# Down projection of a convolutional FFN: 18 of its 22 feature tiles by Strassen's seven products

## The reference

```python
def conv_ffn(x, w_up, conv_w, conv_b, w_down):
    h = x @ w_up                               # 1024 -> 2 * 2816
    h = depthwise conv of width 3 over tokens + conv_b
    a, u = jnp.split(h, 2, axis=-1)
    return (gelu(a) * u) @ w_down              # 2816 -> 1024

x = layer_norm(ALPHA * x + mix, ln1_g, ln1_b)
x = layer_norm(ALPHA * x + conv_ffn(x, ...), ln2_g, ln2_b)
```

## Time and profile before

| what | value |
|---|---|
| time, median of 3 runs | 1003.73 us (1003.02 to 1004.0) |
| span of the profiled execution | 1001.4 us |
| instructions in it | 12301 |
| PE busy | 987.4 us, 99% of the span |
| DVE, ACT, POOL busy | 734.4, 464.8, 220.7 us |
| mean granted TensorE clock | 0.999 |
| moved by DMA | 102.11 MB |

### The profile page before, as it was taken

How to read it: one execution, slowest core, us unless ns; L and a number is a source line. 1 busy time by engine, 2 the same in 40 slices (tenths; PEclk the granted TensorE clock), 3 DMA queues, 4 the chain that set the end, 5 groups by cost and what they waited for, 6 DMA issues and landing times.

```text
span 1001.4 us, 12301 instructions
## 1 busy us (share of the span) xinstructions
PE 987.4 (99%) x4614; PEld 824.2 (82%) x4614; DVE 734.4 (73%) x1110; ACT 464.8 (46%) x742; POOL 220.7 (22%) x210
## 2 busy tenths in 40 slices
PE   7999999999999999999999999999999999999997
PEld 6888888998888788888888888888888888888885
DVE  6664567886786898788778778778777394665587
ACT  6574666896313754554554554454457402113000
POOL 2400426774950000000000000000000299500022
PEclk9999999999999999999999999999999999999999
DMA  8334141008240223223222322322339512413022
GB/s 309 95 81 151 43 107 43 1 1 252 85 148 22 84 65 103 82 68 93 76 85 76 92 85 67 103 85 63 105 134 350 209 72 97 169 53 158 1 84 84
DMA packets 91179, 102.11 MB, mean 102 GB/s; under 512 B 20091, under 2 KB 71247, under 8 KB 91120
## 3 DMA queue, kind: packets, MB, share of 16 engines
q1 hardware_dynamic: 89904, 99.15, 30.0%
q10 hardware_dynamic: 1216, 2.17, 0.7%
HBM read 79.29 MB, written 22.02 MB: 101 GB/s over the span
## 4 chain that ended last, share of the span: by engine, by line
PE 95%; DVE 2%; ACT 2%; issue 1%; DMA 0%; POOL 0%; DVEq 0%; SPq 0%; ACTq 0%; POOLq 0%
PE ps L701 31%; PE ps L703 30%; PE ps L702 30%; PE ps L915 1%; PE ps L1044 1%; DVE prob L1377 1%; DVE pTl L1174 1%; ACT prob L1908 1%; PE ps L736 1%; ACT pTh L1731 0%; DMA acc<-in_x_prompt 0%; PE ps L711 0%; PE ps L724 0%; PE ps L884 0%; PE ps L976 0%
## 5 line engine op out<-in xcount | busy, mean ns | idle before, releaser
L701 PE MATMUL ps<-d_hi,g_hi 128*128 128x512 f32 x352 | 137.0, 389 | 0.0
L703 PE MATMUL ps<-d_hi,g_lo 128*128 128x512 f32 x352 | 136.9, 389 | 0.0
L702 PE MATMUL ps<-d_lo,g_hi 128*128 128x512 f32 x352 | 136.9, 389 | 0.0
L668 POOL TENSOR_TENSOR acc<-acc,gain_bc 128x1024 f32<-128x1024 f32 x12 | 32.8, 2732 | 466.2 <-ACT bias_bc L1731 466.2
L702 PEld LDWEIGHTS ps<-d_lo,g_hi 128*128 128x128 f32 x352 | 66.1, 188 | 13.8
L703 PEld LDWEIGHTS ps<-d_hi,g_lo 128*128 128x128 f32 x352 | 66.1, 188 | 13.8
L701 PEld LDWEIGHTS ps<-d_hi,g_hi 128*128 128x128 f32 x352 | 66.1, 188 | 13.7 <-DVE d_lo L1174 0.2
L701 PE MATMUL ps<-x1h,wa_hi 128*128 128x512 f32 x192 | 75.6, 394 | 0.0
L703 PE MATMUL ps<-x1h,w_lo 128*128 128x512 f32 x192 | 74.8, 389 | 0.0
L702 PE MATMUL ps<-x1l,wa_hi 128*128 128x512 f32 x192 | 74.7, 389 | 0.0
L2028 ACT ACTIVATE hc<-U,taps 128x512 f32<-128x512 f32 x60 | 48.7, 813 | 44.7 <-DVE U L1556 41.4
(11 more groups left out here) (298 smaller groups left out, 2740.4 us busy)
## 6 DMA issues: line engine op xcount, KB each, us to landing
w_raw<-in_w_up SPq DMA_DIRECT2D x44, 512.0 KB, 4.7
g_scratch<-gated SPq DMA_DIRECT2D x22, 512.0 KB, 2.6
g_raw<-g_scratch SPq DMA_DIRECT2D x22, 512.0 KB, 6.1
d_raw<-in_w_down SPq DMA_DIRECT2D x22, 512.0 KB, 7.4
acc<-in_x_sample SPq DMA_DIRECT2D x8, 512.0 KB, 12.0
st_raw<-in_w_in SPq DMA_DIRECT2D x16, 256.0 KB
x_scratch<-acc SPq DMA_DIRECT2D x8, 512.0 KB, 3.5
acc<-x_scratch SPq DMA_DIRECT2D x8, 512.0 KB, 7.9
```

What stands on the lines that cost most here:

```text
L668: chain.mark(pool.tensor_tensor(dst, dst, gain_bc[:], ALU.mult))
L701: pe.matmul(out, whi, xhi, start=start, stop=False, skip_group_check=onto)
L702: pe.matmul(out, whi, xlo, start=False, stop=False, skip_group_check=onto)
L703: return pe.matmul(out, wlo, xhi, start=False, stop=stop, skip_group_check=onto)
```

## The change

For the first 18 feature tiles the down projection is no longer 16 blocks per chunk. The tiles are taken in pairs (one tile is the first, the other the second half of the contraction), the tokens in two sequences and the columns in two halves, so that a pair is a product of 2 x 2 blocks, and it is done by seven products (`PRODUCTS`). Three pairs go together (`CHUNK` = 3), which gives 21 steps (`STEPS`). A step is four token tiles of nine matmuls, in four banks; even and odd steps use different banks. The products' operands are sums: those of gated rows (S1 to S4) are built in DRAM, in `gs_scratch`, and those of weights (T1 to T4) in `ts_scratch`, by transfers that POOL issues and that add to what their target holds (`accum_op`). Plain copies of the first terms are issued by SP. Each step loads 128 x 1536 of either operand into one of five slots (`SLOTS`). The last four tiles (`LAST`) are done as before, in 16 blocks of 12 matmuls.

Added or rewritten, cut to the core:

```diff
+PAIRED = 18
+QUADS = PAIRED // 2
+CHUNK = 3
+STEPS = 7 * (QUADS // CHUNK)
+SLOTS = 5
+LAST = FT - PAIRED
+PRODUCTS = ((X11, B11, True, True), (X12, B21, False, True), (S2, T2, False, False), (S1, T1, False, True),
+            (S3, T3, True, False), (S4, B22, False, False), (X22, T4, True, False))
+TARGETS = ((0, 0, 1), (0, 0, 1), (0, 1, -1), (4, 1, 1), (4, 1, -1), (0, 1, 1), (4, 0, 1))
+def by_act(n):
+    return n in (0, 2, 3, 6)
...
             def store_gated(v):
+                g, q = gated[v % 2], v // 2
                 sp.wait_ge(g_ready, 2 * v + 2)
-                sp.dma_start(g_dram[v], gated[v % 2][:]).then_inc(g_out[v % 2], 16)
...
+                elif v % 2 == 0:
+                    sp.dma_start(gs_dram[X11:S3 + 1, :, q, :].rearrange("i p n -> p i n"),
+                                 g[:, 0:SEQ].unsqueeze(1).to_broadcast([P, 3, SEQ])).then_inc(g_out[0], 16)
+                    sp.dma_start(gs_dram[S1, :, q, :], g[:, SEQ:2 * SEQ]).then_inc(g_out[0], 16)
...
+            def load_step(n):
+                c, i = divmod(n, 7)
+                a, w, s = PRODUCTS[i][0], PRODUCTS[i][1], n % SLOTS
...
+                if n >= SLOTS:
+                    sp.wait_ge(dn_ps, 4 * (n - SLOTS + 1))
+                sp.dma_start(ga_raw[s][:], gs_dram[a, :, quads(c), :]).then_inc(step_in[s], 16)
+                src = ts_dram[TSUM[w], :, quads(c), :] if w in TSUM else quarter[w][:, quads(c), :]
+                sp.dma_start(db_raw[s][:], src).then_inc(step_in[s], 16)
...
                 elif v + 2 < FT:
                     sp.wait_ge(p_ps[3], v + 1 - PLAIN)
                     load_up(v + 2)
+                    if v - PLAIN < 12:
+                        start_weight_sum(v - PLAIN)
                 elif v + 2 == FT:
                     sp.wait_ge(p_ps[3], v + 1 - PLAIN)
...
+                    sp.wait_ge(p_ps[1], FT - PLAIN)
+                    load_step(0)
+                    load_step(1)
+                else:
+                    sp.wait_ge(p_ps[4], FT - PLAIN)
+                    load_step(2)
                 store_gated(v)
             sp.wait_ge(p_ps[3], FT - PLAIN)
+            load_step(3)
+            for s in range(2):
+                sp.wait_ge(g_out[s], 16 * FT)
+            load_step(4)
             for t in range(TT):
                 sp.dma_start(acc[:, t, :], x1_dram[t]).then_inc(x_in[t], 16)
-            sp.wait_ge(dn_ps, 16)
-            for s in range(2):
-                sp.wait_ge(g_out[s], 16 * (FT // 2))
-            load_chunk(2)
             sp.dma_start(gain_bc[:], ln1_g.partition_broadcast(P)).then_inc(gb_in, 16)
             sp.dma_start(bias_bc[:], ln1_b.partition_broadcast(P)).then_inc(gb_in, 16)
...
+            for n in range(SLOTS, STEPS):
+                load_step(n)
...
+            def row_sums(v):
...
+                q = v // 2
+                pool.wait_ge(g_ready, 2 * v + 2)
+                pool.wait_ge(g_out[0], 32 * (q + 1))
+                high = gated[v % 2][:, SEQ:2 * SEQ]
+                if v % 2 == 0:
+                    pool.dma_start(gs_dram[S3, :, q, :], high, accum_op=ALU.add).then_inc(g_sum[0], 16)
+                else:
+                    pool.dma_start(gs_dram[S1, :, q, :], high, accum_op=ALU.add).then_inc(g_sum[1], 16)
+                    pool.wait_ge(g_sum[1], 16 * (q + 1))
+                    pool.dma_start(gs_dram[S2, :, q, :], gs_dram[S1, :, q, :], accum_op=ALU.add).then_inc(gs_sum, 16)
+                    pool.wait_ge(gs_sum, 32 * q + 16)
+                    pool.wait_ge(g_out[1], 32 * (q + 1))
+                    pool.dma_start(gs_dram[S4, :, q, :], gs_dram[S2, :, q, :], accum_op=ALU.add).then_inc(gs_sum, 16)
...
+            def weight_row_sums(c, part):
...
+                if part == 0:
+                    pool.wait_ge(ts_copy, 64 * (c + 1))
+                    pool.dma_start(k[0], b12[:, w, :], accum_op=ALU.add).then_inc(ts_sum, 16)
+                    pool.dma_start(k[2], quarter[B22][:, w, :], accum_op=ALU.add).then_inc(ts_sum, 16)
+                elif part == 1:
+                    pool.wait_ge(ts_sum, 64 * c + 32)
+                    pool.dma_start(k[1], k[0], accum_op=ALU.add).then_inc(ts_sum, 16)
...
+            for v in range(PAIRED):
+                row_sums(v)
+                c, part = divmod(v - 6, 4)
+                if 0 <= c and part < 3:
+                    weight_row_sums(c, part)
...
+            for n in range(STEPS):
+                for t in range(TB):
+                    if by_act(n):
+                        take_step(n, t)
+                    if t % 2 and n + 2 < STEPS:
+                        step_high(n + 2, t // 2)
+                if n == 0:
                     act.wait_ge(gb_in, 64)
                     copy(gain_bc[:], gain_bc[:], gb_ready, ALPHA)
                     copy(bias_bc[:], bias_bc[:], gb_ready, ALPHA)
...
+            lows = [(0, 0), (0, 1), (1, 0), (1, 1), (2, 0), (2, 1), (3, 0), (3, 1)]
+            for n in range(STEPS):
+                for t in range(TB):
+                    if not by_act(n):
+                        add_step(n, t)
+                    if t % 2 and n + 2 < STEPS:
+                        step_low(n + 2, t // 2)
+                    elif n + 2 == STEPS and t == 3:
+                        last_low(0, 0)
+                        last_low(0, 1)
+                    elif n + 1 == STEPS:
+                        if t == 1:
+                            for j, w in lows[2:5]:
+                                last_low(j, w)
+                        elif t == 3:
+                            for j, w in lows[5:8]:
+                                last_low(j, w)
```

More of the change, by code:

```diff
@@ L309, in build @@
-    d_his = [[t[:] for t in d_hi_t[s]] for s in range(2)]
-    for tiles, n, dt, o in ((g_raws, "g_raw4", F32, 84), (g_los, "g_lo4", F32R, 84), (d_raws, "d_raw4", F32, 88), (d_los, "d_lo4", F32R, 88),
-                            (g_his, "g_hi4", F32R, 92), (d_his, "d_hi4", F32R, 96)):
-        tiles[0].append(at(n, [P, D], dt, R + o * KB)[:])
+    part_sum = at("part_sum", [P, TT, D], F32, R + 98 * KB)
+    SLOT_KB = ((22, 28, 34, 40), (46, 60, 92, 52), (68, 74, 80, 86), (130, 136, 142, 148), (0, 6, 12, 154))
@@ L464, in _ @@
             sp.wait_ge(proj_ps, 2 * TILES)
-            sp.wait_ge(ssf_ps, 1)
+            sp.wait_ge(ss_ps, 1)
             load_wo(0)
@@ L1134, in _, with down_step @@
             product(FT - 1, 3)
-            def down(c, i):
+            def down_step(n):
+                i, s = n % 7, n % SLOTS
+                fresh = PRODUCTS[i][3]
+                for t in range(TB):
+                    if n >= 2:
+                        act_took, count = taken(n - 2, t)
+                        pe.wait_ge(dn_act if act_took else dn_dve, count)
+                    elif n == 0 and t == 2:
+                        pe.wait_ge(conv_done, 4 * (FT - 2) + 3)
+                    elif n == 0 and t == 3:
+                        pe.wait_ge(c11_sum, FT - PLAIN - 1)
+                    elif n == 1 and t == 0:
+                        pe.wait_ge(c12_sum, FT - PLAIN - 1)
+                    elif n == 1 and t == 1:
+                        pe.wait_ge(conv_done, 4 * (FT - 1) + 3)
+                    elif n == 1 and t == 2:
+                        pe.wait_ge(c11_sum, FT - PLAIN)
+                    elif n == 1 and t == 3:
+                        pe.wait_ge(c12_sum, FT - PLAIN)
+                    if t == 0:
+                        pe.wait_ge(dn_lo, 2 * n + 2)
+                    tok = slice(t * P, (t + 1) * P)
+                    for q in range(CHUNK):
+                        last = mm3(ps[:, DOWN_BANKS[n % 2][t], :], ga_hi[s][:, q, tok], ga_lo[s][:, q, tok], db_hi[s][:, q, :], db_lo[s][:, q, :],
+                                   fresh and q == 0, q == CHUNK - 1, not fresh)
+                    last.then_inc(dn_ps, 1)
@@ L1163, in down @@
                 last.then_inc(dn_ps, 1)
-            for c in range(len(CHUNKS)):
-                for i in range(16):
-                    down(c, i)
+            for n in range(STEPS):
+                down_step(n)
+            for i in range(2 * TT):
+                down_last(i)
         @block.vector
@@ L1676, in _, with add_step @@
                 up_tail(v)
-            def add_down(c, i):
+            def add_step(n, t):
+                first, half, sign = TARGETS[n % 7]
+                dst = part_sum[:, first + t, half * 512:(half + 1) * 512]
+                dve.wait_ge(dn_ps, 4 * n + t + 1)
+                act_took, count = taken(max(k for k in range(n) if TARGETS[k % 7][0:2] == (first, half)), t)
+                dve.wait_ge(dn_act if act_took else dn_dve, count)
+                dve.tensor_tensor(dst, dst, ps[:, DOWN_BANKS[n % 2][t], :], ALU.add if sign > 0 else ALU.subtract).then_inc(dn_dve, 1)
@@ L1679, in add_down, with add_last @@
+            def add_last(i):
                 t, half = divmod(i, 2)
                 cols = slice(half * 512, (half + 1) * 512)
```

(19 more changed lines are left out.)

335 lines of the change are left out of this document (173 added, 162 removed).

## The result

The changed kernel takes 1062.2 us (median of 4 runs, 1061.6 to 1063.1), the kernel before 1003.7 us (4 runs on the same chip, 1003.0 to 1004.0). The ratio is 1.058, 95% interval 1.057 to 1.060: slower by 58.5 us. The forecast was 1020 us, 1002 to 1033. The side was right and the size was not: 42 us are missing, and the time lies 28 us above even the dearest rival (1034).

The account below looks back on a forecast made before the run. PE, busy 99% of the span, was taken as the bound. Terms -24.5 + 0.8 + 17.3 + 13.4 + 2.4 + 5 + 2 = +16.4 us on 1001.4 gave 1017.8, plus 2.3 to the median: 1020 us, range 1002 to 1033.

Parts of the forecast that it names:

- The removed matmuls: Down stage: 948 matmuls instead of 1056, 108 fewer at 0.2267 us each, -24.5 us.
- step 1: Start of the down stage: its weights' high part comes late behind the last GELU, +0.8 us, bounds 0.5 and 2.
- the wait for gain and bias: Down stage, step 3: ACT waits for both loads before making its high parts, so PE starts late, +17.3 us, 13 to 19.
- The last four tiles: End of the down stage: PE waits for low parts that take turns with POOL's `part_sum` additions, +13.4 us; lower bound 2.6.
- that bound as +2.4 us: Last blocks: DVE needs 5.79 us per token tile, PE 5.44, so DVE ends +2.4 us behind after seven distances.
- The up stage: Up stage: POOL's adding transfers and SP's copies delay weight loads that have 1.1 us of cover, +5 us, bounds 0 and 19.
- The prediction's own sign of being wrong: Up stage: adding transfers that each take much more than 5 us would show the prediction wrong.
- The argument for the lower end: Up stage: +5 us was taken nearer 0 than 19 because stores and loads already share the queue without harm.
- rival 1: Up stage: adding transfers hold up weight loads to their upper end, +19 us instead of +5, giving 1034 us; chance 0.12.
- The clock: After both long down-stage waits: PE restarts at the 1.2 GHz level, +2 us for the two together.
- that gain and bias might land early: Down stage, step 3: both loads land by 778, so it waits under 8 us; 1003 us with no wait; chance 0.12.
- that there might be no turns: Last tiles and step 3: waits of 2.6 and 15.4 us, nothing lost in the up stage, 1001 us; chance 0.06.

Follow-up runs that it names:

- run c: Changed kernel, with ACT waiting for gain and bias after the fourth step instead of the first: 1043.9 us.
- run d: Changed kernel, with POOL adding `part_sum` only after DVE's last low parts are made: 1060.6 us.
- run i: Changed kernel, with POOL adding `part_sum` only after DVE's last low parts and `rstd` of tile t placed behind the addition of tile t+2: 1057.1 us.
- run q: Changed kernel: weight adds spread, gain/bias wait later, last low parts two by two, POOL's `part_sum` additions after them, `rstd` interleaved, later additions waiting for DVE's earlier rows: 995.1 us.
- runs a: Changed kernel without POOL's twelve adding transfers of weights, with SP's copies and the rows' sums kept: 1019.4 us.
- run b: Changed kernel with the same twelve weight transfers made plain copies that add nothing: 1031.4 us.
- run k: Kernel before, with only the change's twelve copies and twelve adding transfers of weights put into its up stage: 1009.6 us.
- run m: Kernel before with the twelve weight copies and adding transfers, the latter issued later, behind the tile's fourth product: 1043.8 us.
- run l: Changed kernel, with POOL issuing the weights' adding transfers ahead of the rows' instead of behind them: 1030.6 us.

## Why the prediction was right and wrong

- **The removed matmuls, step 1, and the wait for gain and bias** held: 108 fewer; a wait of 0.94 us at step 1; 15.6 us at step 3, worth 18.3 by run c. Counted from the start of the down stage, gain and bias landed 1.5 us sooner than worked out.
- **The last four tiles** held as a wait, 11.7 for 13.4 us, and by its mechanism: DVE and POOL take turns (low parts of 2.6 to 3.4 us beside POOL, 1.21 alone). But its 13.4 us were not there to be won. Runs d and i return 1.6 and 5.1 us, because the next thing is late at once: in run d `rstd`, in run i DVE, whose token tiles are the bound of the last blocks and which now meets POOL's additions there. The prediction had that bound as +2.4 us by itself and should have read the two terms as one.
- **That the down stage came out at +12.1 for +11.4 is in part luck.** Its two waits were 3.4 us shorter than in the sum, and what DVE and the end add behind the last matmul was 1.3 us for 2.4. The slow clock made up for it: its term was +2, and PE's slow matmuls there cost about 6 us (from the first matmul of the stage to the last it is 250.1 us, of which 214.7 are the full-clock distances of 948 matmuls and 29.5 the waits, counted over those distances).
- **The up stage is the step that failed**: "I take +5 us", with an upper bound of 19, measured 45.7. Its reasoning had the right place and the right cover (1.1 us, nothing given back) and three wrong inputs. *The rate*: 0.37 MB per us comes from plain loads. Adding transfers ran at 0.16; reading the target too, which I had as the upper bound, would have been 0.185, near it. *The issue*: I let the adding transfers "follow" the store, 9 us after the load. They wait for the store to land and follow it by POOL's order, 15.7 us after the load, and those of the next tile 27.7 us after theirs, when the next load is issued. At the measured rate that puts the end of the pair at 488.7 + 11.5 = 500.2, 7.6 us into the next load; the interval grew by 8.66. *The second collision*: that of the next tile was taken as up to 3 us and measured 5.5 to 6.9. The row chain of an odd tile ends only when the next load is issued, even where nothing is disturbed (434.88 for the load at 434.70), so the 0.79 MB behind it start just as that load does. The prediction's own sign of being wrong was there too: each of the pair took 12.0 us from issue to landing, not 5.
- **The argument for the lower end** ("stores and loads share the queue in every stage now without harm") was wrong in kind. In the trace of before a store is issued 9 us after a load and 10 us before the next, so the two never meet. It showed no contention because it had no overlap, and it could not price one.
- **The rule of the Trainium skill** that I kept as rival 1 (page "DMA: Bandwidth & Descriptors", section "Issuing engines are not separate DMA queues": transfers of all engines run on the same 16 DMA engines and interleave) agrees with the trace: the load of 1 MB at 492.58 served DVE after 13.9 us instead of 5.75, in slices where the engines are full with POOL's transfers. It was given a chance of 0.12, and the time it was given was too small as well.
- **The clock**, +2 us for two waits: run c's 18.3 against a wait of 15.6 gives 2.7 for the first alone. In the up stage PE lost about 46 us, of which 30.5 are the waits themselves; the rest is mostly the slow matmuls after them. The sum had no term for that, since it had no wait there.
- **The rivals**: that gain and bias might land early, and that there might be no turns, are both refuted by the rows above.

## What to carry to other kernels

A transfer that is cheap on average can be the dearest thing in the kernel if it meets a load with 1 us of cover: ask when it is *issued*, which follows from the last wait ahead of it in its engine's program, and whether it ends before the next such load. Price a new kind of transfer by its own rate, not by that of plain loads, and do not take the absence of harm from a trace in which the two never overlap. Before moving an operation away from a shared resource, read what is next in line on both engines: the edit at the last tiles took 9 us from PE's waits and made the kernel only 1.6, then 5 us faster, and only its third form (run q) kept POOL out of DVE's way there too.

## What the runs showed of the hardware

- Twelve adding transfers from DRAM to DRAM, 9.44 MB, took 56 us of all 16 DMA engines (0.17 MB per us), and the same twelve made plain 28 us (0.34), by the shares of q0 in the changed kernel and in runs a and b; run k has 56 us for them too. The kernel with the plain ones was 31 us faster.
- The same twelve cost 6 us when their pair was issued 6.6 us before a weight load (run k) and 41 us when it was issued 2.0 us before it (run m).
- While adding transfers filled the DMA engines, SP's own issue was held up: copies that take about 1.1 us to issue took 6.6 us here and 7.5 us in run m. In run k the copy took 4.2 us, and little was lost.
- After the waits of 3.6 to 7 us in the up stage PE restarted at 1.2 GHz: the first matmul took 0.79 us for 0.39 at full clock, and the granted clock was 0.50. Shorter waits differ. After one of 2.81 us in run l the granted clock stayed at 1.00; after two of 2.2 and 2.3 us in run b it was 0.71 and 1.00, and no run here shows what decides between them. The wait of 2.79 us at the last tiles had two longer ones ahead of it with three slow matmuls after each, so its 0.50 is no measure of a short wait.
- Beside POOL's addition DVE's operations with two SBUF operands of 1024 columns wait for its turn (2.5 for 1.28 us), and its sums from PSUM and its statistics do not (0.68 and 0.69 us).
